# First stage of a decoder trunk on one core: x loaded in four pieces, the norm by token halves, V begun with two units, scale columns finished on ScalarE

## The chip, the core and the metric

One core of a Trainium2 chip runs the whole program. The metric is the device time of one execution in microseconds (us); of several runs the median counts. Engines are called as the profile calls them: PE (TensorE, matmuls), ACT (ScalarE), DVE (VectorE), POOL (GpSimd), SP (SyncE, which issues all DMAs here). They run side by side, each through its own list of instructions in order, and meet only at semaphores.

## What is computed

Two layers of a decoder on x (512 tokens, 1024 features), float32. Cut to what the change touches:

```
mod = c_act @ w_ada[l] + b_ada[l]           # c_act = silu(c); gives sh1, sc1, g1, sh2, sc2, g2
h = rms_norm(x, norm1_g[l]) * (1.0 + sc1) + sh1
proj = h @ w_in[l]                          # conv parts, q, k, v, gate
...                                         # convolution, retention, output projection, MLP
```

with `rms_norm(x, g) = x * rsqrt(mean(x*x) + EPS) * g`. Everything after the first h is unchanged.

## The kernel before

**Layout.** x lies transposed in SBUF: 128 partitions of features, 8 tiles k of 128 features (KT = 8), 512 tokens. A float32 product is made of three matmuls of rounded parts: each operand is split in a high part (a cast to fp32r, on ACT) and a low part (full minus high, a subtraction), and high*high, high*low and low*high are added up in PSUM. So a weight block w_raw[:, j] (128x1024, four slots j, called units) needs a cast to w_hi on ACT and a subtraction to w_lo on DVE or POOL before PE can use it.

**First stage.** The SP queue loads, in order: c and the identity, x in two pieces of 1 MB (`load_x`), bias and parameters between them, then blocks of 512 KB: the modulation weights of tile 0 (scale, shift), the weight units 0 and 1, the scale block of tile 1, the units 2 and 3, the shift block of tile 1, and then scale and shift of the tiles 2 to 7. After the last it waits until all four w_lo are done before it issues the second round of weights.

**Norm.** ACT squares the eight tiles of x (L756), DVE adds them up in `ssum` (L1170), PE takes the mean over features (L386, four small matmuls), ACT the root (L706), DVE the reciprocal (L1217), ACT writes it as diagonal blocks (L788), and PE spreads it over all partitions (L393) into the bank `rinv` of PSUM. Between the fourth and the fifth square ACT copies c_act out of PSUM (L760); POOL's and DVE's work on the modulation waits for that.

**h, tile by tile.** For tile k, DVE multiplies the scale block with c and sums it (L1177, 128x1024), forms the gain from it (L1184), and multiplies x, gain and rinv into `xr` in PSUM (L1194). The shift block is multiplied on POOL (L1584; of tile 0 on DVE, L1213) and summed on ACT (L769, L772). ACT adds the shift and rounds to h_hi (L779), DVE forms h_lo (L1199). In a loop DVE's order is product(k), scale(k+1), gain(k+1), low(k), as `xr` is a single buffer.

**V.** PE begins with V: for each tile k, four token tiles t times three matmuls of 512 columns, all four units at once (`v_tile`, L402 to L404), into the banks 0 to 3. It waits for all four w_lo and for h_lo of tile k. Tile 7 comes in two passes of two units (256 columns). Then the other projections follow (L360 to L362), whose weights are split meanwhile.

**The four weight splits** of the first round: the casts on ACT (L764), the subtractions of units 0, 1 and 3 on POOL (L1579) and of unit 2 on DVE (L1207). POOL has its seven shift blocks behind them.

What sets the order around the change is the text of each engine's list; nothing is scheduled by a planner.

## Time and profile before

| | us |
|---|---|
| median of 3 runs (1164.0 to 1164.42) | 1164.42 |
| the profiled execution | 1164.55 |
| its span, first to last instruction | 1162.6 |
| PE busy | 1133.8 |
| DVE busy | 847.9 |
| ACT busy | 564.2 |
| POOL busy | 183.7 |

The profile is of one execution. The span leaves out 1.95 us (1164.55 less 1162.6) around it. PE is busy for 98% of the span; what it lacks lies almost wholly in the first of 40 slices. A busy share is an average, so the stage in question is read instruction by instruction.

### The profile page before, as it was taken

The page shows a single profiled execution, that of the slowest core. Times are in us where ns is not written, and L with a number is a line of the kernel's source. Part 1 is how long each engine was busy: PE and PEld are TensorE (multiplying, and loading weights), DVE is VectorE, ACT ScalarE, POOL GpSimd, SP SyncE. Part 2 cuts the span into 40 slices and gives each one's busy share as a digit, 9 for nine tenths or more (in the row PEclk, how much of TensorE's full clock was granted, in tenths as well). Part 3 has the DMA queues.
Part 4 walks back from the last instruction along what each step waited for, and adds up shares of the span by engine and source line. Part 5 has one row for each costly group of instructions (what it writes and reads, how often), then busy time and mean ns, then how long its engine had stood idle before and what let it go on. Part 6 is the DMA issues. An engine that isn't in the chain of part 4 may idle for free.

```text
span 1162.6 us, 18883 instructions
## 1 busy us (share of the span) xinstructions
PE 1133.8 (98%) x6650; PEld 1003.3 (86%) x6650; DVE 847.9 (73%) x1275; ACT 564.2 (49%) x941; POOL 183.7 (16%) x140
## 2 busy tenths in 40 slices
PE   4999999999999999999999999999999999999996
PEld 2788888998989989989998888889989989999896
DVE  6966887779778687685577678786897575775754
ACT  5654444347445454454444544434555454544631
POOL 4495010320000000000215801004000000000003
PEclk9999999999999999999999999999999999999998
DMA  9774334624443353433345433452323232232312
GB/s 351 305 289 145 126 108 145 217 74 136 137 159 113 128 161 126 143 114 104 128 158 214 162 126 121 150 204 98 118 101 127 85 109 97 90 126 72 109 54 73
DMA packets 47059, 162.84 MB, mean 140 GB/s; under 512 B 5536, under 2 KB 7712, under 8 KB 46752
## 3 DMA queue, kind: packets, MB, share of 16 engines
q1 hardware_dynamic: 47008, 162.18, 40.4%
q8 instruction: 30, 0.49, 0.2%
q14 instruction: 21, 0.17, 0.0%
HBM read 160.06 MB, written 2.10 MB: 139 GB/s over the span
## 4 chain that ended last, share of the span: by engine, by line
PE 93%; DVE 3%; ACT 1%; DMA 1%; issue 1%; SPq 1%; POOL 0%; POOLq 0%; DVEq 0%; ACTq 0%
PE ps L360 21%; PE ps L361 21%; PE ps L362 21%; PE ps L516 8%; PE ps L518 8%; PE ps L517 8%; PE ps L611 1%; PE ps L402 1%; DVE h_lo L1068 1%; PE ps L596 1%; DMA w_raw<-weights 1%; PE ps L403 1%; PE ps L404 1%; DVE x L1105 1%; DVE x L1133 0%
## 5 line engine op out<-in xcount | busy, mean ns | idle before, releaser
L989 DVE TENSOR_TENSOR w_lo<-w_raw,w_hi 128x1024 fp32r<-128x1024 f32 (+1 forms) x190 | 226.8, 1195 | 195.1 <-ACT w_hi L691 193.5
L691 ACT CAST w_hi<-w_raw 128x1024 fp32r<-128x1024 f32 (+1 forms) x190 | 189.2, 997 | 80.5 <-PE ps L362 69.5
L360 PE MATMUL ps<-u_hi,w_hi 128*128 128x512 f32 (+1 forms) x576 | 211.4, 367 | 0.0
L361 PE MATMUL ps<-u_lo,w_hi 128*128 128x512 f32 (+1 forms) x576 | 210.8, 366 | 0.0
L362 PE MATMUL ps<-u_hi,w_lo 128*128 128x512 f32 (+1 forms) x576 | 210.5, 365 | 0.0
L360 PE MATMUL ps<-h_hi,w_hi 128*128 128x512 f32 (+1 forms) x528 | 194.6, 368 | 0.8 <-DVE h_lo L1068 0.8
L362 PE MATMUL ps<-h_hi,w_lo 128*128 128x512 f32 (+1 forms) x528 | 192.0, 364 | 0.0
L361 PE MATMUL ps<-h_lo,w_hi 128*128 128x512 f32 (+1 forms) x528 | 191.9, 364 | 0.0
L1566 POOL TENSOR_TENSOR ssum<-ssum,buf_a 128x256 f32<-128x256 f32 (+1 forms) x56 | 51.9, 926 | 772.0 <-ACT buf_a L719 769.2
L1133 DVE SCALAR_TENSOR_TENSOR x<-ps,mod,x 128x512 f32<-128x512 f32 (+1 forms) x168 | 105.4, 668 | 35.6 <-PE ps L362 35.6
L362 PEld LDWEIGHTS ps<-u_hi,w_lo 128*128 128x128 f32 x576 | 108.7, 189 | 17.7
L360 PEld LDWEIGHTS ps<-u_hi,w_hi 128*128 128x128 f32 x576 | 108.7, 189 | 16.9
L361 PEld LDWEIGHTS ps<-u_lo,w_hi 128*128 128x128 f32 x576 | 108.8, 189 | 16.6
L360 PEld LDWEIGHTS ps<-h_hi,w_hi 128*128 128x128 f32 x528 | 99.6, 189 | 16.9 <-DVE h_lo L1068 1.6
L362 PEld LDWEIGHTS ps<-h_hi,w_lo 128*128 128x128 f32 x528 | 99.6, 189 | 15.8
L361 PEld LDWEIGHTS ps<-h_lo,w_hi 128*128 128x128 f32 x528 | 99.7, 189 | 15.1
L887 ACT CAST s_hi<-s_full 128x512 fp32r<-128x512 f32 x104 | 63.3, 619 | 75.8 <-DVE s_full L1381 73.4
L516 PE MATMUL ps<-t_hi,s_hi 128*128 128x256 f32 x312 | 88.4, 283 | 0.0
L518 PE MATMUL ps<-t_hi,s_lo 128*128 128x256 f32 x312 | 88.3, 283 | 0.0
L517 PE MATMUL ps<-t_lo,s_hi 128*128 128x256 f32 x312 | 88.3, 283 | 0.0
L1000 DVE CUSTOM_DVE_ANT_0 ada_raw<-ada_raw,c_act 128x1024 f32<-128x1024 f32 x56 | 68.6, 1241 | 3.3 <-DMA ada_raw<-ada 2.9
L1385 DVE TENSOR_TENSOR s_lo<-s_full,s_hi 128x512 fp32r<-128x512 f32 x104 | 66.7, 683 | 0.0
(189 smaller groups left out, 2282.4 us busy)
## 6 DMA issues: line engine op xcount, KB each, us to landing
w_raw<-weights SPq DMA_DIRECT2D x200, 512.0 KB, 3.4
ada_raw<-ada SPq DMA_DIRECT2D x80, 512.0 KB, 4.8
arena<-ada SPq DMA_DIRECT2D x16, 512.0 KB, 15.2
x<-xT SPq DMA_DIRECT2D x2, 1024.0 KB, 6.8
tab<-tables SPq DMA_DIRECT2D x2, 1024.0 KB, 14.6
outT<-x SPq DMA_DIRECT2D x8, 256.0 KB, 2.3
tab<-tables SPq DMA_DIRECT2D x1, 512.0 KB, 14.9
ident<-identity SPq DMA_DIRECT2D x1, 64.0 KB, 2.0
```

Of the source, the lines that this page charges most:

```text
L360: nc.tensor.matmul(out, wh, hi, start=first, stop=False, skip_group_check=True)
L361: nc.tensor.matmul(out, wh, lo, start=False, stop=False, skip_group_check=True)
L362: return nc.tensor.matmul(out, wl, hi, start=False, stop=last, skip_group_check=True)
L516: nc.tensor.matmul(out, wh, high(k), start=first and k == 0, stop=False, skip_group_check=True)
L517: nc.tensor.matmul(out, wh, low(k), start=False, stop=False, skip_group_check=True)
L518: mm = nc.tensor.matmul(out, wl, high(k), start=False, stop=k == 3, skip_group_check=True)
L691: nc.scalar.copy(w_hi[:, j, cols], w_raw[:, j, cols]).then_inc(w_hi_done, 1)
L887: nc.scalar.copy(s_hi[:, at, :], s_full[:, at, :]).then_inc(s_hi_done, 1)
L989: nc.vector.tensor_tensor(w_lo[:, j, cols], w_raw[:, j, cols], w_hi[:, j, cols].bitcast(F32), ALU.subtract).then_inc(w_lo_done, 1)
L1000: nc.vector.tensor_tensor_reduce(out=ada_raw[:, slot, :], in0=ada_raw[:, slot, :], in1=by, scale=1.0, scalar=0.0, op0=ALU.mult, op1=ALU.ad ...
L1133: nc.vector.scalar_tensor_tensor(out=xm, in0=ps[:, bank, at], scalar=mod[:, bass.ds(m + gate_col, 1)], in1=xm, op0=ALU.mult, op1=ALU.add). ...
L1385: nc.vector.tensor_tensor(s_lo[:, at, :], s_full[:, at, :], s_hi[:, at, :].bitcast(F32), ALU.subtract).then_inc(s_split, 1)
```

## The change

x comes in four pieces of two tiles (512 KB), and the host lays it out so that a partition's two tiles are contiguous (4 KB runs instead of 2 KB). The shift block of tile 1 is loaded ahead of the units 2 and 3.

The last two tiles of x are squared and added in halves of 256 tokens, and mean, root, reciprocal, diagonal and spreading are done for each half. The diagonal is now written by DVE (`first_diag`, a multiplication of the identity with the reciprocal, both in SBUF), where ACT did it. The c_act copies move behind the last square on ACT.

POOL begins with the shift block of tile 0, does the subtraction of unit 0 only, and goes on with the shifts of the tiles 1 to 7. DVE does the subtractions of the units 1, 2 and 3, between the steps of the tiles 0 to 2, and no longer the shift block of tile 0. The gains of the tiles 1 to 7 are formed on ACT from the sum (`first_gain`).

Tile 0 of h is made by halves, with its product in SBUF (`xr_first`), not in PSUM. PE does the tiles 0 and 1 of V for the units 0 and 1 first (256 columns, as soon as w_lo of these two is there: `first_lo`), then, when all four are there, the same tiles for the units 2 and 3, then the tiles 2 to 7 as before. SP waits for `first_lo` too before the second round of weights.

```diff
-        xr = ps[:, STAT, :]
+        pair_banks = ps[:, STAT:RMS + 1, :].rearrange("p a t -> p (a t)")
+        first_rinv_all = pair_banks[:, T // 2:T // 2 + T]
+        first_rinv_at = [first_rinv_all[:, at] for at in HALVES]
+        first_stats = [pair_banks[:, 0:2], pair_banks[:, T + T // 2:T + T // 2 + 2]]
+        xr = ps[:, STAT:RMS + 1, :].rearrange("p a (h t) -> p (a h) t", h=2)[:, ::3, :]
+        xr_first = buf_a[:, 0, :]
...
-                sp.dma_start(x[:, 4 * i:4 * i + 4, :], xT[4 * i:4 * i + 4, :, :].rearrange("k p t -> p k t")
-                             ).then_inc(x_in[i], 16)
+                sp.dma_start(x[:, 2 * i:2 * i + 2, :], xT[:, 2 * i:2 * i + 2, :]).then_inc(x_in[i], 16)
...
-            load_x(0)
-            sp.dma_start(bia[:], bias).then_inc(par_in, 16)
-            sp.dma_start(par[:], params).then_inc(par_in, 16)
-            load_x(1)
+            def load_first(j):
+                sp.dma_start(w_raw[:, j, :], weights[j, :, :]).then_inc(w_in[j], 16)
+
+            for i in range(4):
+                load_x(i)
+                if i == 1:
+                    sp.dma_start(bia[:], bias).then_inc(par_in, 16)
+                    sp.dma_start(par[:], params).then_inc(par_in, 16)
             load_scale(0)
             load_shift(0)
-            for j in range(SLOTS):
-                sp.dma_start(w_raw[:, j, :], weights[j, :, :]).then_inc(w_in[j], 16)
-                if j == 1:
-                    load_scale(1)
-            for k in range(1, KT):
+            load_first(0)
+            load_first(1)
+            load_scale(1)
+            load_shift(1)
+            load_first(2)
+            load_first(3)
+            for k in range(2, KT):
+                load_scale(k)
                 load_shift(k)
-                if k + 1 < KT:
-                    load_scale(k + 1)
             sp.dma_start(fin_g[:], final_g).then_inc(fin_in, 16)
+            sp.wait_ge(first_lo, 2)
...
-            pe.wait_ge(x_added, KT - 1)
-            mean_squares(0, 0, 0, TOKEN_TILES)
-            spread(0, 1, WHOLE)
+            for half in range(2):
+                pe.wait_ge(x_added, KT - 1 + 2 * half)
+                for i in range(2):
+                    t = 2 * half + i
+                    mm = nc.tensor.matmul(first_stats[half][:, i:i + 1], ssum[:, t * P:(t + 1) * P], mean_d[:],
+                                          start=True, stop=True, skip_group_check=True)
+                mm.then_inc(stat_ps if half else first_stat, 1)
+            for half in range(2):
+                pe.wait_ge(norm_r if half else first_r, 2)
+                nc.tensor.matmul(first_rinv_at[half], ones[:], ssum[:, HALVES[half]], start=True, stop=True,
+                                 skip_group_check=True).then_inc(rinv_ps if half else first_rinv, 1)
             pe.wait_ge(c_ready, 2)
             pe.wait_ge(mean_ready, 1)
 
+            pe.wait_ge(first_lo, 2)
+            for t in range(TOKEN_TILES):
+                if t % 2 == 0:
+                    pe.wait_ge(xs_lo, t // 2 + 1)
+                v_tile(0, t, (0, 2), True, False)
+            pe.wait_ge(xs_lo, 4)
+            for t in range(TOKEN_TILES):
+                v_tile(1, t, (0, 2), False, False)
             pe.wait_ge(w_lo_done, 2 * SLOTS)
             for k in range(KT):
                 pe.wait_ge(xs_lo, 2 * k + 2)
                 if k < KT - 1:
                     for t in range(TOKEN_TILES):
-                        v_tile(k, t, (0, SLOTS), k == 0, False)
+                        v_tile(k, t, (2 if k < 2 else 0, SLOTS), False, False)
...
+            act.wait_ge(x_in[3], 16)
+            for half, at in enumerate(HALVES):
+                for m in (KT - 2, KT - 1):
+                    act.wait_ge(x_added, m - 4 + 2 * half)
+                    first_square(m, (m + 2 * half) % 4, at)
+            for i in range(2):
+                act.wait_ge(c_ps, i + 1)
+                nc.scalar.copy(c_act[:, HALVES_D[i]], ps[:, 6 + i, :]).then_inc(c_ready, 1)
...
+            def first_gain(k):
+
+                act.wait_ge(sc_summed, k + 3)
+                nc.scalar.activation(gm[:, 0, k:k + 1], sc_sum[:, k:k + 1], ACT.Identity, bias=sc_gain[:, k:k + 1],
+                                     scale=par[:, C_G1 + k:C_G1 + k + 1]).then_inc(gm_ready, 1)
+
             act.wait_ge(par_in, 32)
+            for half in range(2):
+                act.wait_ge(stat_ps if half else first_stat, 1)
+                nc.scalar.activation(std[:, 2 * half:2 * half + 2], first_stats[half], ACT.Sqrt, bias=eps[:, 0:1]
+                                     ).then_inc(norm_std if half else first_std, 1)
             first_split(0)
+            first_shift(0)
             first_split(1)
-            norm_root(0, 1, TOKEN_TILES)
-            act.wait_ge(norm_r, 1)
-            for t in range(TOKEN_TILES):
-                diag = nc.scalar.activation(ssum[:, t * P:(t + 1) * P], ident[:], ACT.Copy, scale=rstd[:, t:t + 1])
-            diag.then_inc(norm_r, 1)
+            act.wait_ge(sh_ready, 1)
+            for half, at in enumerate(HALVES):
+                act.wait_ge(xr_ready if half else first_xr, 1)
+                nc.scalar.activation(h_hi[:, 0, at], xr_first[:, at], ACT.Identity, bias=mod[:, 0:1]).then_inc(xs_hi, 1)
+            first_gain(1)
             first_split(2)
+            first_shift(1)
+            first_high(1)
             first_split(3)
-            first_high(0)
-            for k in range(1, KT):
+            for k in range(2, KT):
+                first_gain(k)
                 first_shift(k)
                 first_high(k)
...
+            for half, at in enumerate(HALVES):
+                for i in range(2):
+                    dve.wait_ge(x_squared, KT - 1 + 2 * half + i)
+                    dve.wait_ge(x_added, KT - 3 + 2 * half + i)
+                    nc.vector.tensor_tensor(ssum[:, at], ssum[:, at], squared[(2 + i + 2 * half) % 4][:, at], ALU.add
+                                            ).then_inc(x_added, 1)
...
+            def first_diag(half):
+
+                step = norm_r if half else first_r
+                t0 = 2 * half
+                dve.wait_ge(norm_std if half else first_std, 1)
+                nc.vector.reciprocal(rstd[:, t0:t0 + 2], std[:, t0:t0 + 2]).then_inc(step, 1)
+                dve.wait_ge(step, 1)
+                nc.vector.tensor_tensor(ssum[:, HALVES[half]].rearrange("p (a b) -> p a b", b=P),
+                                        ident[:].unsqueeze(1).to_broadcast([P, 2, P]),
+                                        rstd[:, t0:t0 + 2].unsqueeze(2).to_broadcast([P, 2, P]), ALU.mult
+                                        ).then_inc(step, 1)
...
+            dve.wait_ge(sc_summed, 1)
+            nc.vector.tensor_tensor(sc_gain[:], sc_bias[:], par[:, C_G1:C_G1 + KT], ALU.mult).then_inc(sc_summed, 1)
+            dve.wait_ge(c_ready, 2)
             first_scale(0)
-            first_gain(0)
-            dve.wait_ge(sh_in[0], 16)
-            nc.vector.tensor_tensor_reduce(out=arena[:, 0, :], in0=arena[:, 0, :], in1=c_row,
-                                           scale=1.0, scalar=0.0, op0=ALU.mult, op1=ALU.add,
-                                           accum_out=sh_sum[:, 0:1]).then_inc(sh_summed, 1)
-            dve.wait_ge(norm_std, 1)
-            nc.vector.reciprocal(rstd[:], std[:]).then_inc(norm_r, 1)
-            dve.wait_ge(sh_summed, 1)
-            nc.vector.tensor_scalar(mod[:, 0:1], sh_sum[:, 0:1], bia[:, 0:1], None, ALU.add).then_inc(sh_ready, 1)
+            first_diag(0)
+            first_diag(1)
+            dve.wait_ge(sc_summed, 3)
+            nc.vector.tensor_scalar(gm[:, 0, 0:1], sc_sum[:, 0:1], sc_bias[:, 0:1], par[:, C_G1:C_G1 + 1],
+                                    ALU.add, ALU.mult).then_inc(gm_ready, 1)
+            dve.wait_ge(gm_ready, 1)
+            for half, at in enumerate(HALVES):
+                dve.wait_ge(rinv_ps if half else first_rinv, 1)
+                nc.vector.scalar_tensor_tensor(out=xr_first[:, at], in0=x[:, 0, at], scalar=gm[:, 0, 0:1],
+                                               in1=first_rinv_at[half], op0=ALU.mult, op1=ALU.mult
+                                               ).then_inc(xr_ready if half else first_xr, 1)
             first_scale(1)
-            first_gain(1)
-            first_split(2)
-            first_product(0)
-            first_low(0)
-            for k in range(1, KT):
+            for half, at in enumerate(HALVES):
+                dve.wait_ge(xs_hi, half + 1)
+                nc.vector.scalar_tensor_tensor(out=h_lo[:, 0, at], in0=xr_first[:, at], scalar=mod[:, 0:1],
+                                               in1=h_hi[:, 0, at].bitcast(F32), op0=ALU.add, op1=ALU.subtract
+                                               ).then_inc(xs_lo, 1)
+            first_split(1, first_lo)
+            first_product(1)
+            first_split(2, w_lo_done)
+            first_low(1)
+            first_scale(2)
+            first_split(3, w_lo_done)
+            for k in range(2, KT):
                 first_product(k)
                 if k + 1 < KT:
                     first_scale(k + 1)
-                    first_gain(k + 1)
                 first_low(k)
...
+            pool.wait_ge(c_ready, 2)
+            first_shift(0)
             first_split(0)
-            first_split(1)
-            first_split(3)
-            pool.wait_ge(c_ready, 2)
             for k in range(1, KT):
...
-        "xT": np.asarray(x)[0].T.reshape(KT, P, T),
+        "xT": np.asarray(x)[0].T.reshape(KT, P, T).transpose(1, 0, 2),
```

Where instructions stand now. The list of POOL before, from its first weight subtraction on (L1579 subtraction of a unit, L1584 shift block of a tile):

```order
L1579 TENSOR_TENSOR w_lo<-w_raw,w_hi 128x1024 [waits w_hi_done] x3
L1584 TENSOR_TENSOR arena<-arena,c_act 128x1024 [waits sh_in1,c_ready]
L1584 TENSOR_TENSOR arena<-arena,c_act 128x1024 [waits sh_in2]
L1584 TENSOR_TENSOR arena<-arena,c_act 128x1024 [waits sh_in3]
L1584 TENSOR_TENSOR arena<-arena,c_act 128x1024 [waits sh_in4]
```

and of the changed kernel (L1656 shift block, L1651 subtraction of unit 0):

```order
L1656 TENSOR_TENSOR arena<-arena,c_act 128x1024 [waits sh_in0,c_ready]
L1651 TENSOR_TENSOR w_lo<-w_raw,w_hi 128x1024 [waits w_hi_done]
L1656 TENSOR_TENSOR arena<-arena,c_act 128x1024 [waits sh_in1]
L1656 TENSOR_TENSOR arena<-arena,c_act 128x1024 [waits sh_in2]
L1656 TENSOR_TENSOR arena<-arena,c_act 128x1024 [waits sh_in3]
```

Two subtractions left POOL, one shift block came, and it stands first.

The list of DVE before, from the first scale block to the product of tile 1 (L1177 scale block, L1184 gain, L1213 shift block, L1207 subtraction of unit 2, L1194 product, L1199 low part):

```order
L1177 ISA arena,sc_sum<-arena,ps 128x1024 [waits sc_in0,c_ready]
...
L1213 ISA arena,sh_sum<-arena,ps 128x1024 [waits sh_in0]
L1213 ISA sh_sum 128x1
L1217 RECIPROCAL rstd<-std 128x4 [waits norm_std]
...
L1184 TENSOR_SCALAR gm<-sc_sum,sc_bias,par 128x1 [waits sc_summed]
L1207 TENSOR_TENSOR w_lo<-w_raw,w_hi 128x1024 [waits w_hi_done]
L1194 SCALAR_TENSOR_TENSOR ps<-x,gm,ps 128x512 [waits gm_ready,rinv_ps]
L1199 SCALAR_TENSOR_TENSOR h_lo<-ps,mod,h_hi 128x512 [waits xs_hi]
L1194 SCALAR_TENSOR_TENSOR ps<-x,gm,ps 128x512 [waits gm_ready,xs_lo]
```

and of the changed kernel, from the second diagonal on (L1243 diagonal half, L1283 product half and L1289 low half of tile 0, L1232 scale block, L1251 subtraction, L1259 product, L1265 low part):

```order
L1243 TENSOR_TENSOR ssum<-ident,rstd 128x256 [waits norm_r]
...
L1283 SCALAR_TENSOR_TENSOR buf_a<-x,gm,ps 128x256 [waits first_rinv,gm_ready]
L1283 SCALAR_TENSOR_TENSOR buf_a<-x,gm,ps 128x256 [waits rinv_ps]
L1232 ISA arena,sc_sum<-arena,ps 128x1024 [waits sc_in1]
...
L1289 SCALAR_TENSOR_TENSOR h_lo<-buf_a,mod,h_hi 128x256 [waits xs_hi] x2
L1251 TENSOR_TENSOR w_lo<-w_raw,w_hi 128x1024 [waits w_hi_done]
L1259 SCALAR_TENSOR_TENSOR ps<-x,gm,ps 128x2x256 [waits gm_ready]
L1251 TENSOR_TENSOR w_lo<-w_raw,w_hi 128x1024 [waits w_hi_done]
L1265 SCALAR_TENSOR_TENSOR h_lo<-ps,mod,h_hi 128x512 [waits xs_hi]
L1232 ISA arena,sc_sum<-arena,ps 128x1024 [waits sc_in2]
...
L1251 TENSOR_TENSOR w_lo<-w_raw,w_hi 128x1024 [waits w_hi_done]
```

Three subtractions now stand between DVE's steps of the tiles 0 to 2, where one stood, and the diagonal and the low halves of tile 0 read two SBUF operands.

## Rows read from the trace of the kernel before

**Rows 1.** The page: PE's busy tenths in 40 slices, and the chain by engine.
```profile
PE   4999999999999999999999999999999999999996
...
PE 93%; DVE 3%; ACT 1%; DMA 1%; issue 1%; SPq 1%; POOL 0%; POOLq 0%; DVEq 0%; ACTq 0%
```

**Rows 2.** Timeline, first 25 us (start us, us, engine, line, operation [idle before <-releaser]).
```profile
9.61 1.05 ACT L760 COPY c_act<-ps 128x512 f32<-128x512 f32 x2
...
10.88 2.15 ACT L756 ACTIVATE ps<-x 128x512 f32<-128x512 f32 x4 [0.21 <-DMA x<-xT]
...
11.51 3.06 DVE L1170 TENSOR_TENSOR ssum<-ssum,ps 128x512 f32<-128x512 f32 x4 [0.49 <-ACT ps L756]
...
14.78 1.04 ACT L764 CAST w_hi<-w_raw 128x1024 fp32r<-128x1024 f32 x1 [1.75 <-DMA w_raw<-weights]
...
18.79 2.08 PE L393 MATMUL ps<-ssum,ones 128*128 128x512 f32 x2 [2.29 <-ACT ssum L788]
...
24.12 0.77 PE L402 MATMUL ps<-w_hi,h_hi 128*128 128x512 f32 x1 [3.25 <-DVE h_lo L1199]
```

**Rows 3.** Timeline: DVE instructions beside POOL instructions, two places.
```profile
15.90 4.67 POOL L1579 TENSOR_TENSOR w_lo<-w_raw,w_hi 128x1024 fp32r<-128x1024 f32 x2 [15.45 <-ACT w_hi L764]
15.94 1.21 DVE L1213 CUSTOM_DVE_ANT_0 arena<-arena,ps 128x1024 f32<-128x1024 f32 x1
...
19.71 1.95 DVE L1207 TENSOR_TENSOR w_lo<-w_raw,w_hi 128x1024 fp32r<-128x1024 f32 x1 [0.74 <-ACT w_hi L764]
...
20.97 2.90 POOL L1579 TENSOR_TENSOR w_lo<-w_raw,w_hi 128x1024 fp32r<-128x1024 f32 x1 [0.39 <-ACT w_hi L764]
...
239.08 2.40 POOL L1571 TENSOR_TENSOR w_lo<-w_raw,w_hi 128x1024 fp32r<-128x1024 f32 x1 [5.70 <-ACT w_hi L691]
239.40 2.37 DVE L1068 SCALAR_TENSOR_TENSOR h_lo<-xr_all,mod,h_hi 128x256 fp32r<-128x256 f32 x1 [0.18 <-ACT h_hi L712]
```

**Rows 4.** All eight diagonal halves on DVE, by line: duration ns min/median/max.
```profile
L1041 DVE TENSOR_TENSOR ssum<-ident,rstd x8: 424/424/715, 235.8 to 1154.9; 128x256 f32<-128x256 f32 x8
```

**Rows 5.** Two shift loads by line, tiles 0 and 2: issue, then landing.
```profile
L282 SPq DMA_DIRECT2D arena<-ada x1: 451/451/451, 4.4 to 4.4; - x1
...
DMA to landing us min/median/max: 9.0/9.0/9.0
...
L282 SPq DMA_DIRECT2D arena<-ada x1: 527/527/527, 8.8 to 8.8; - x1
...
DMA to landing us min/median/max: 14.8/14.8/14.8
```

**Rows 6.** Busy time by window, last columns: PE clock granted, DMA share, GB/s.
```profile
6.50:7.00 0.50, 0.50 (x2) 0.17 (x1) 0.00 (x0) 0.00 (x0) 0.00 (x0) 1.00 1.04 336
...
11.00:11.50 0.50, 0.00 (x0) 0.00 (x0) 0.03 (x1) 0.50 (x2) 0.00 (x0) 1.00 1.00 410
```

**Rows 7.** Timeline, 25 to 50 us: PE's steps and one DVE product and gain.
```profile
25.54 0.63 PE L402 MATMUL ps<-w_hi,h_hi 128*128 128x512 f32 x1
25.97 0.63 PE L403 MATMUL ps<-w_lo,h_hi 128*128 128x512 f32 x1
...
32.30 0.76 DVE L1194 SCALAR_TENSOR_TENSOR ps<-x,gm,ps 128x512 f32<-128x512 f32 x1
32.31 0.50 PE L402 MATMUL ps<-w_hi,h_hi 128*128 128x512 f32 x1
...
34.22 0.27 DVE L1184 TENSOR_SCALAR gm<-sc_sum,sc_bias,par 128x1 f32<-128x1 f32 x1
...
43.87 0.50 PE L402 MATMUL ps<-w_hi,h_hi 128*128 128x512 f32 x1
44.21 0.40 PE L403 MATMUL ps<-w_lo,h_hi 128*128 128x512 f32 x1
...
46.72 0.28 PE L402 MATMUL ps<-w_hi,h_hi 128*128 128x256 f32 x1
...
49.59 0.40 PE L360 MATMUL ps<-h_hi,v_hi 128*128 128x512 f32 x1
```

64 lines of the change are left out of this document (30 added, 34 removed).

## The prediction

> **What bounds the kernel now.** I read the page first: PE is at nine tenths in every slice but the first and the last, and makes up 93% of the chain that ended last [rows 1]. So nothing after the first 50 us can be won by this change, and what the first stage gains or loses passes through whole, as a shift. The measure of the stage is the moment at which PE leaves V and starts the next projection: 49.59 us [rows 7]. Then the timeline of the first 25 us: the last four squares start at 10.88, when the second half of x has landed, the last sum is ready at 14.57 (11.51 + 3.06), the spreading ends at 20.87, V begins at 24.12 after 3.25 us of idle PE [rows 2]. Then V itself: matmuls of 512 columns come every 0.43 us at first (25.54 to 25.97: the 1.2 GHz level) and every 0.228 later (44.21 to 46.72 for eleven of them: the 2.4 GHz level). Tile 2 begins at 32.31 and tile 7 at 46.72, so a tile takes 2.88, though PE needs only 12 x 0.228 = 2.74 [rows 7]: DVE paces it, by 0.14 per tile.
>
> **Which resource decides.** Two places show DVE and POOL standing in each other's way. At 239.40 DVE's low half takes 2.37 us while a POOL subtraction runs from 239.08 to 241.48, and ends 0.29 after it; all eight diagonal halves lie between 0.424 and 0.715 us, so 0.47 is what such an instruction needs alone [rows 3, 4]. At 19.71 DVE's subtraction takes 1.95 and ends 1.09 after POOL's second one (15.90 + 4.67 = 20.57); POOL's third then takes 2.90 instead of 2.34 and ends 2.21 after DVE's [rows 3]. But DVE's block product at 15.94, which has one operand in PSUM, takes 1.21 in the middle of a POOL instruction [rows 3]. So: a DVE instruction with two SBUF inputs waits for the running POOL instruction to end, and POOL's next waits for it. Reading from these rows, a held subtraction ends 1.1 after POOL's end, and POOL's next ends 2.2 after that. The changed kernel gives DVE three such subtractions, two diagonals and two low halves at a time in which POOL, with its shift blocks first, is hardly idle. That is the heart of this prediction.
>
> **Part 1, the loads.** While x comes in, the queue moves 336 GB/s at a full DMA share, and 410 later [rows 6]. x's runs become as long as the other blocks'. The 2.1 MB of x take 6.2 us at the one rate and 5.1 at the other, so all that follows lands between 0 and 1.1 us earlier; I take 0.8, nearer the later row, because the later blocks have just these runs. The last of x then lands at 10.1 instead of 10.88. Shift block 0 landed at 4.4 + 9.0 = 13.4 and shift block 2 at 8.8 + 14.8 = 23.65 [rows 5]; their places in the queue stay, so 12.6 and 22.85.
>
> **Part 2, the norm.** After x's last piece there were four squares and sums left, 3.7 us to the last sum. Now four halves: a sum of 512 columns takes 0.77 (3.06 / 4), a half about 0.43 (a diagonal half's 0.424, [rows 4]), and DVE is still at the fifth sum until 11.0. So the first half's sum is ready at 11.9 and the second's at 12.7. Mean and root end at 14.15 for the second half (an estimate: about 0.95 for two of the four small matmuls, 0.3 for the root). The c_act copies, 1.05 us [rows 2], now stand last on ACT and end at 12.5, which costs nothing, since shift block 0 lands at 12.6.
>
> **Part 3, the chain through POOL.** POOL's shift 0 runs 12.6 to 15.0. DVE's scale 0 ends at 14.1; its first diagonal is ready at 14.2, is held and ends at 15.3. ACT casts unit 0 from 14.15 to 15.2 (1.04, [rows 2]), so POOL takes its subtraction at 15.2, and DVE's second diagonal asks at 15.4, too late by about 0.2: it ends at 17.9, not 15.8. Spreading a half: 1.04 to 2.08, half of the whole's 2.08 [rows 2] or all of it; I take 1.2, as its columns halve. It ends at 19.1, the second product half at 19.7, scale 1 at 20.8, both low halves at 21.6, DVE's subtraction of unit 1 at 22.7 (POOL is idle here: shift 1 done at 20.2, shift 2 not landed). V begins at 22.8, 1.3 earlier than now.
>
> **Part 4, the chain to the second pair of units.** DVE makes product 1 (0.76, [rows 7]) until 23.4 and then asks for the subtraction of unit 2. POOL began shift 2 at 22.9, when it landed, and ends at 25.2. The subtraction ends at 26.3, POOL's shift 3 at 28.5. Low 1 ends at 27.0, scale 2 at 28.1, the subtraction of unit 3 is held until 28.5 and ends at 29.6. Only then are all four w_lo there. PE: tile 0 for two units, 12 steps of half 0.43, 22.8 to 25.3; idle; tile 1 at 27.05 to 29.6 at the low clock; the second pair from 29.7. Its 24 steps of 0.12 ((49.59 - 46.72) / 24, [rows 7]) are 2.87, and 0.3 more for what is still at the low clock, so tile 2 begins at 32.9. That is 0.6 **later** than the 32.31 of now, though V began 1.3 earlier.
>
> **Part 5, the gains on ACT.** They take 0.27 from DVE's loop [rows 7]; its 2.88 falls to 2.6 or 2.7, below PE's 2.74. The next limit is PE itself. ACT has 2.5 us of work per tile with it (an estimate from its shift, high and gain steps), which is below 2.74. Five tiles at 2.74 are 13.7 instead of 14.41, a gain of 0.7; without this cover being complete the gain lies between 0 and 0.7. Tile 7 keeps its 2.87.
>
> **Part 6, the second round of weights.** SP waits now until 29.6 (it issued at 23.9), but blocks landed 15 us after their issue [rows 5], so the queue is filled to about 36 and the wait costs nothing; it would cost from a wait until 34 on.
>
> **The sum.** 32.9 + 13.7 + 2.87 = 49.5 against 49.59: **-0.1 us**. The profiled execution has 1164.55, of which 1.95 outside the span; it lies 0.13 above the median, 1164.42. On the median's side: 1164.3, rounded to **1164.4**, no change. What moves it inside this case: the loads 0 to 1.1 earlier (+0.8 to -0.3), the gain's cover (+0.7 to 0), the clock in the idle places (-0.3 to +1.2).
>
> **Rival A, the order flips.** In Part 4 DVE asks 0.4 us after POOL has begun shift 2, in Part 3 0.2 us after POOL has begun unit 0. If DVE comes first at the second place (or at the first, which brings the spreading 2 us forward and DVE most of the 0.4), the subtraction of unit 2 ends at 24.5, shift 2 at 26.7, low 1 at 25.2, scale 2 at 26.4, and the subtraction of unit 3 at 27.8. The second pair starts at 27.85 at full clock and tile 2 at 30.7: 2.3 earlier than in the forecast, so 1162.1. For it: both margins are smaller than what the estimates of Part 2 and 3 leave open. Against: both would have to be wrong in the same direction, as the landings shift both sides alike. Chance 0.24, half of it beyond 0.2%.
>
> **Rival B, no waiting.** If these operands don't hold DVE, subtractions end where they are asked for: unit 1 at 20.6, unit 3 at 25.4, tile 2 at 28.4, 4.5 earlier than in the forecast: 1159.9. Against it stand rows 3 and 4. The Trainium skill speaks for waiting too: "SBUF — State Buffer", "Who interferes with whom", says that a DVE instruction with two SBUF inputs contends with a GpSimd one that reads SBUF and that the order of issue decides who blocks. By that rule this rival falls and the forecast or rival A is left. Chance 0.05.
>
> **Rival C, slower: PE's clock falls back.** V's start now has two idle places, 1.7 us after tile 0 and, if tile 1 runs at the high level, 1.2 before the second pair. Before, it had one of 0.74 behind tile 0, and stayed at the high level after it, which it reached 3.2 us after V began. The point from which it decides is whether PE is still at the low level at 29.7. Then a climb of 3.2 us at half speed costs 1.6, of which 0.3 is in the sum: +1.2, 1165.6; with loads that gain nothing besides, +2.0; only a second climb brings it past 0.2%. The Trainium skill ("TensorE: Matmul & The Clock Gate", "What's actually happening") has the low rate as the default that activity releases; by it the three short bursts are a worse start than one long one. No row shows what 1.7 us of idle do. Chance 0.12, of which 0.06 past 0.2%.
>
> **Rival D.** That the change does not do what it says, for instance x in 4 KB runs out of a source with a longer pitch between them gaining nothing or losing: then all lands as now and the time is 1165.1. It is inside the forecast's own range.
>
> **How the numbers follow.** Forecast case 0.59, with its own range of 1163.5 to 1165.6; A 0.24 at 1162.1; C 0.12 at 1165.6 and up; B 0.05 at 1159.9. A measurement of this kernel can tell about 0.2% (2.3 us) from no change. Faster by more: half of A, B and a rest, 0.20. Slower by more: 0.06. Same: 0.74. For 8 in 10 the range takes in most of A and of C: 1161.7 to 1166.0.
>
> **What would show it.** In the profile of the changed kernel: V's first matmul near 22.8; DVE subtractions of the units 2 and 3 of more than 1.9 us each, ending just behind POOL shift blocks; the second diagonal held by more than 1.5 us; the second pair's first matmul (256 columns) near 29.7; tile 2 near 32.9 and then tiles of 2.74; the next projection at 49.5. Rival A shows the subtraction of unit 2 at its 1.2 us and POOL's shift 2 longer instead. B shows three subtractions of 1.2. C shows steps of 0.21 us for 256 columns after 30. I would be wrong, too, if PE were seen waiting again between the tiles 3 and 7, or if the loads of x landed later than 10.9.

## The result, and the profile after

| | before | changed |
|---|---|---|
| median, 15 runs each (us) | 1164.42 (1163.75 to 1164.83) | 1170.99 (1165.76 to 1172.93) |
| ratio, 95% interval | | 1.0058 (1.0051 to 1.0065) |
| the profiled execution | 1164.55 | 1172.48 |
| its span | 1162.6 | 1170.7 |

**Slower by 0.58%.** The forecast was no change, and the range ended at 1166.0, so it was wrong. The runs of the changed kernel lie in two groups, 1170.4 to 1171.1 and 1172.2 to 1172.9, and one at 1165.76; the profile is of the upper one. What parts them stays open.

The page of the changed kernel: PE's tenths and the granted clock in 40 slices, and the chain by engine.

```profile
PE   2999999999999999999999999999999999999996
...
PEclk6899999999999999999999999999999999999998
...
PE 93%; DVE 5%; ACT 1%; DMA 1%; issue 0%; SPq 0%; POOL 0%; POOLq 0%; DVEq 0%; ACTq 0%
```

As in [rows 1], all but the first slice is PE's. That slice fell from 4 to 2 tenths, and DVE's part of the chain rose from 3% to 5%. So the place to look is the first 50 us, and DVE in it. The timeline of that stretch, changed kernel (start us, us, engine, line, operation [idle before <-releaser]):

```profile
10.97 1.30 ACT L786 ACTIVATE ps<-x 128x256 f32<-128x256 f32 x4 [0.19 <-DMA x<-xT]
...
13.64 2.34 POOL L1656 TENSOR_TENSOR arena<-arena,c_act 128x1024 f32<-128x1024 f32 x1 [13.20 <-DMA arena<-ada]
13.80 2.22 DVE L1270 TENSOR_SCALAR sc_bias<-bia 128x8 f32<-128x8 f32 x1
...
17.52 1.37 DVE L1243 TENSOR_TENSOR ssum<-ident,rstd 128x256 f32<-128x256 f32 x1
...
19.00 2.37 DVE L1243 TENSOR_TENSOR ssum<-ident,rstd 128x256 f32<-128x256 f32 x1
...
23.81 2.35 POOL L1656 TENSOR_TENSOR arena<-arena,c_act 128x1024 f32<-128x1024 f32 x1 [2.72 <-DMA arena<-ada]
...
24.23 4.77 DVE L1289 SCALAR_TENSOR_TENSOR h_lo<-buf_a,mod,h_hi 128x256 fp32r<-128x256 f32 x2
26.38 2.34 POOL L1656 TENSOR_TENSOR arena<-arena,c_act 128x1024 f32<-128x1024 f32 x1 [0.22 <-DMA arena<-ada]
28.92 1.21 DVE L1251 TENSOR_TENSOR w_lo<-w_raw,w_hi 128x1024 fp32r<-128x1024 f32 x1
...
30.39 0.55 PE L419 MATMUL ps<-w_hi,h_hi 128*128 128x256 f32 x1 [7.74 <-DVE w_lo L1251]
30.71 2.76 DVE L1251 TENSOR_TENSOR w_lo<-w_raw,w_hi 128x1024 fp32r<-128x1024 f32 x1
...
35.20 1.60 DVE L1251 TENSOR_TENSOR w_lo<-w_raw,w_hi 128x1024 fp32r<-128x1024 f32 x1
...
40.59 0.40 PE L419 MATMUL ps<-w_hi,h_hi 128*128 128x512 f32 x1
```

What to see, in order:

- The squares behind the last piece of x start at 10.97, where they started at 10.88 [rows 2].
- **sc_bias**, eight numbers per partition out of one SBUF tile, takes 2.22 us. It begins 0.16 after POOL's shift block and ends 0.04 after it (16.02 to 15.98). Nothing in the prediction speaks of it. In the kernel before it stood between the sums, with POOL idle until 15.90 [rows 3]:

```profile
10.86 0.16 DVE L1166 TENSOR_SCALAR sc_bias<-bia 128x8 f32<-128x8 f32 x1
```

- Scale block and diagonals follow two microseconds late, and the second diagonal is held to 21.37 by shift block 1.
- The two **low halves** of tile 0 ask at 24.23. Shift block 2 has started at 23.81, so the first is held to 26.2, and shift block 3 holds the second to 29.0. Together they take 4.77 us; where nothing holds them they take 0.88 (e1 below).
- V starts at 30.39 instead of 24.12 [rows 2], after 7.74 us of idle PE. Subtractions of the units 2 and 3 are held too. Tile 2 starts at 40.59 instead of 32.31, and V is left at 57.09 instead of 49.59 [rows 7]: **7.5 us later**. The span grew by 8.1; the other 0.6 lies behind V.

Busy time by window of the changed kernel; the last three columns are the granted PE clock, the DMA share and GB/s:

```profile
28.00:32.00 4.00, 1.61 (x7) 1.64 (x8) 4.00 (x4) 1.12 (x2) 3.78 (x2) 0.50 1.03 410
32.00:36.00 4.00, 3.10 (x15) 2.80 (x14) 4.00 (x5) 1.20 (x3) 4.00 (x3) 0.50 0.78 304
36.00:40.00 4.00, 4.00 (x26) 3.98 (x25) 3.96 (x7) 3.09 (x7) 4.00 (x2) 0.68 0.52 181
```

DVE is busy for all of 28 to 36 and PE is not; DVE's held instructions count as busy. The PE clock is at its lower level, 1.2 GHz, up to the third of these windows, and V's steps of 256 columns came every 0.21 us until about 38.5, then every 0.12. The DMA queue begins to run dry behind 32 (its share falls to 0.78, then 0.52), as SP waits for the last w_lo and issues the second round at 36.88.

### The profile page after: what moved, and what is told of

It is laid out like the page before. It is cut to its first block, busy times and chain, and to the rows that moved or that the text cites. A ratio compares the mean times of both kernels' runs of the same rounds, so it can differ in the third digit from the quotient of the medians.

```text
span 1170.7 us, 18946 instructions
## 1 busy us (share of the span) xinstructions
PE 1135.7 (97%) x6676; PEld 1007.8 (86%) x6676; DVE 859.5 (73%) x1275; ACT 567.3 (48%) x951; POOL 183.5 (16%) x139
## 4 chain that ended last, share of the span: by engine, by line
PE 93%; DVE 5%; ACT 1%; DMA 1%; issue 0%; SPq 0%; POOL 0%; POOLq 0%; DVEq 0%; ACTq 0%
PE ps L377 21%; PE ps L378 21%; PE ps L379 21%; PE ps L533 7%; PE ps L535 7%; PE ps L534 7%; PE ps L644 1%; PE ps L419 1%; DVE h_lo L1121 1%; PE ps L420 1%; PE ps L421 1%; PE ps L629 1%; DMA x<-xT 1%; DVE x L1158 1%; DVE x L1186 0%
```

## The experiments

**Theory H:** POOL holds DVE. One small instruction, sc_bias, was held where the prediction counted nothing, and that pushed the low halves under the shift blocks 2 and 3. **Rivals:** the low clock of PE at V's start; the shape of V's start (two units first). A profile is of one execution, which can lie a microsecond or more beside its kernel's median; where that matters it is said. All kernels were compared with the kernel before on the same chip, whose median lay between 1164.24 and 1164.48 in every comparison.

### One part undone at a time

**e1**: sc_bias and sc_gain stand before the fourth sum.

```diff
             for m in range(1, KT - 2):
+                if m == 4:
+                    dve.wait_ge(par_in, 32)
+                    nc.vector.tensor_scalar(sc_bias[:], bia[:, 1:2 * KT:2], 1.0, None, ALU.add).then_inc(sc_summed, 1)
+                    ...
                 dve.wait_ge(x_squared, m + 1)
...
-            dve.wait_ge(par_in, 32)
-            nc.vector.tensor_scalar(sc_bias[:], bia[:, 1:2 * KT:2], 1.0, None, ALU.add).then_inc(sc_summed, 1)
```

> The changed kernel, with the two small DVE instructions for sc_bias and sc_gain back ahead of the fifth sum, where POOL is idle. Theory (a DVE instruction whose operands need the path shared with POOL waits for the running POOL instruction): sc_bias takes 0.16 us instead of 2.22, the diagonals are asked for 2 us earlier but the second is still held, V starts at 23.5 to 24.5 instead of 30.4 because the low halves now come before shift 2 lands, PE leaves V at about 51 instead of 57.1; time 1166. Rival (the stage is longer because of the loads or of the low PE clock alone): V starts 0 to 2 us earlier than 30.4, time 1170 to 1173.

Measured: 1165.69, ratio 1.0008 (0.9998 to 1.0018). Its timeline:

```profile
9.62 0.17 DVE L1219 TENSOR_SCALAR sc_bias<-bia 128x8 f32<-128x8 f32 x1
...
22.12 0.88 DVE L1290 SCALAR_TENSOR_TENSOR h_lo<-buf_a,mod,h_hi 128x256 fp32r<-128x256 f32 x2
...
24.15 2.38 POOL L1657 TENSOR_TENSOR arena<-arena,c_act 128x1024 f32<-128x1024 f32 x1 [2.67 <-DMA arena<-ada]
24.39 0.55 PE L419 MATMUL ps<-w_hi,h_hi 128*128 128x256 f32 x1 [3.84 <-DVE w_lo L1256]
```

Moving two instructions of 0.17 us gave 5.3 of the 6.6 us back (1165.69 against 1170.99, by medians). The low halves now ask at 22.12, two microseconds before shift block 2, and take 0.88. Tile 2 starts at 34.25 and V is left at 50.75.

**e2**: tile 0's product lies in PSUM, so that the low halves have one SBUF input.

```diff
-        xr_first = buf_a[:, 0, :]
+        xr_first = [pair_banks[:, 0:T // 2], pair_banks[:, T + T // 2:2 * T]]
```

> The changed kernel, with the product of tile 0 in PSUM, so that the two low halves of tile 0 read one SBUF operand. Theory: they take 0.48 us each instead of 4.77 together; the subtraction of unit 1 may be held once instead; V starts 3 to 5 us earlier, at 25.5 to 27.5, and PE leaves V near 54; time 1167 to 1169. Rival (the halves were long for another reason, such as waiting for ACT): they stay above 2 us.

Measured: 1168.66, ratio 1.0040 (1.0025 to 1.0054); V starts at 27.48 and is left at 53.92.

```profile
23.79 2.35 POOL L1655 TENSOR_TENSOR arena<-arena,c_act 128x1024 f32<-128x1024 f32 x1 [2.62 <-DMA arena<-ada]
...
24.30 0.87 DVE L1288 SCALAR_TENSOR_TENSOR h_lo<-ps,mod,h_hi 128x256 fp32r<-128x256 f32 x2
25.09 2.13 DVE L1251 TENSOR_TENSOR w_lo<-w_raw,w_hi 128x1024 fp32r<-128x1024 f32 x1
```

Asked at nearly the same moment as in the changed kernel (24.30 and 24.23), both low halves take 0.87 with POOL running: with an operand in PSUM they aren't held. The hold goes to the subtraction behind them.

**e3**: the diagonals are written by ACT, the reciprocals come before scale block 0.

```diff
+                for t in (2 * half, 2 * half + 1):
+                    diag = nc.scalar.activation(ssum[:, t * P:(t + 1) * P], ident[:], ACT.Copy, scale=rstd[:, t:t + 1])
...
-                nc.vector.tensor_tensor(ssum[:, HALVES[half]].rearrange("p (a b) -> p a b", b=P),
-                                        ...
```

> The changed kernel, with the two diagonals written by ACT (two instructions of 128 columns for each half) and the reciprocals ahead of the first scale block on DVE. Theory: no diagonal is held, spreading is done at 18.5 instead of 22.65; then the subtraction of unit 1 or the low halves meet shift 2 and V starts at 24 to 27.5, PE leaves V between 51 and 54; time 1166 to 1169. Rival: V starts within 1 us of 30.4.

Measured: 1169.85, ratio 1.0046 (1.0029 to 1.0062). V starts at 28.04 and is left at 55.04, later than expected.

```profile
21.83 2.67 DVE L1289 SCALAR_TENSOR_TENSOR h_lo<-buf_a,mod,h_hi 128x256 fp32r<-128x256 f32 x2 [0.49 <-ACT h_hi L844]
...
24.33 2.37 POOL L1656 TENSOR_TENSOR arena<-arena,c_act 128x1024 f32<-128x1024 f32 x1 [0.51 <-DMA arena<-ada]
...
24.42 3.36 DVE L1251 TENSOR_TENSOR w_lo<-w_raw,w_hi 128x1024 fp32r<-128x1024 f32 x1
```

The low halves meet shift block 1 now, and the subtraction of unit 1 comes 0.09 after shift block 2 has started. A hold that is taken away is followed by the next one. The edit has a price of its own too: ACT's diagonals stand ahead of its cast of unit 0, POOL waited 2.63 us for that cast, and shift block 1 started at 21.47 instead of 18.69.

**e5**: e1, e2 and e3 together.

> The changed kernel with all three edits at once: sc_bias and sc_gain early, the diagonals on ACT, the product of tile 0 in PSUM. Theory: only the three weight subtractions on DVE can still be held; V starts between 23.2 and 24.5 instead of 30.4, PE leaves V between 47.8 and 49 (49.59 before the change), time 1162.5 to 1164. Rival (the edits are worth no more together than the best of them alone, which left V at 50.75): time 1165 or more.

Measured: 1163.82, ratio 0.9995 (0.9986 to 1.0005). In the profile V starts at 23.43 but is left at 49.95, not at 49 or before; all three subtractions are still held (2.33, 3.33 and 1.62 us). The profiled execution, 1164.92, is 1.1 above the median.

### Is POOL the cause?

**e4**: POOL writes the shift blocks' product area without reading (the shift is left out of h).

```diff
-                nc.gpsimd.tensor_tensor(arena[:, 2 * k, :], arena[:, 2 * k, :], c_act[:], ALU.mult
-                                        ).then_inc(sh_product, 1)
+                nc.gpsimd.memset(arena[:, 2 * k, :], 0.001).then_inc(sh_product, 1)
```

> The changed kernel, with POOL's eight shift products replaced by plain writes of the same blocks (the shift is then left out of the result), so that POOL reads no SBUF there. Theory: every DVE instruction of the first stage goes back to its own duration (sc_bias 0.16, diagonals 0.42, low halves 0.48, subtractions 1.2), except beside POOL's one subtraction; V starts near 21.6, PE leaves V near 46 to 47; time 1161 to 1162. Rival (writes hold DVE too, or the waits come from elsewhere): the long durations stay and V starts after 27.

Measured: 1163.05, ratio 0.9987 (0.9978 to 0.9997); V starts at 23.71 and is left at 48.09.

```profile
13.19 0.95 POOL L1656 MEMSET arena<- 128x1024 f32 x1 [12.74 <-DMA arena<-ada]
13.39 0.78 DVE L1270 TENSOR_SCALAR sc_bias<-bia 128x8 f32<-128x8 f32 x1
...
23.36 0.95 POOL L1656 MEMSET arena<- 128x1024 f32 x1 [4.16 <-DMA arena<-ada]
...
24.03 1.22 DVE L1251 TENSOR_TENSOR w_lo<-w_raw,w_hi 128x1024 fp32r<-128x1024 f32 x1
```

All three subtractions take 1.22 now. Only the one shown met a memset: they share 0.28 us, and it wasn't held. The whole loss, and more, hangs on POOL's eight shift blocks; as they are also shorter here (0.95 instead of 2.35), the run doesn't say how much is the reading and how much the length. V starts later than the 21.6 expected, since the second diagonal met POOL's subtraction of unit 0 and took 2.38 us. And sc_bias is held even by an instruction that only writes: it ends 0.03 after the memset.

### Which forms are held

**e11** and **e13** add DVE instructions of 128x8 whose results nobody uses.

```diff
+                if k == 2:
+                    nc.vector.tensor_scalar(probe[:, 0:KT], bia[:, 1:2 * KT:2], 1.0, None, ALU.add)
+                    ...
```

> The changed kernel with five DVE instructions of 128x8 elements more, whose results nobody uses, beside POOL's row of shift blocks (about 28 to 42 us): two behind the product of tile 2 (add of a constant, with a source of every second element, as sc_bias; the same with a contiguous source), three behind the product of tile 3 (add and multiply with scalars per partition; a plain copy; a product of two SBUF tiles). Alone each takes about 0.17 us. The theory that POOL holds every form that DVE can run at its fast rate or that has two SBUF inputs expects the two adds of a constant, the copy and the product of two tiles to be held up to 2.3 us (ending with a POOL instruction), and the form with scalars per partition perhaps not, as the gains of 128x1 took 0.27. The rule on which the prediction rested expects only the product of two tiles to be held. A third theory, that the source of every second element is slow, expects only the first.

Measured, one run: 1172.59. The first, sc_bias over again, took 1.72 us at 37.12, with POOL running. The second stood right behind it (0.16), and the other three came after POOL's last shift block had ended at 41.15 (0.28, 0.17, 0.16). Inconclusive for these four; so e13 puts its forms where POOL runs for certain:

```diff
+            dve.wait_ge(sh_in[0], 16)
+            dve.wait_ge(c_ready, 2)
+            nc.vector.tensor_scalar(probe[:, 2 * KT:3 * KT], bia[:, 0:KT], eps[:, 0:1], eps[:, 0:1], ALU.add, ALU.mult)
+            nc.vector.tensor_copy(probe[:, 3 * KT:4 * KT], bia[:, 0:KT])
             nc.vector.tensor_scalar(sc_bias[:], bia[:, 1:2 * KT:2], 1.0, None, ALU.add).then_inc(sc_summed, 1)
...
             first_scale(0)
+            nc.vector.tensor_scalar(probe[:, KT:2 * KT], bia[:, 0:KT], 1.0, None, ALU.add)
```

> The changed kernel with three DVE instructions of 128x8 more whose results nobody uses: in front of sc_bias, just after POOL has begun shift block 0, an add and multiply with scalars per partition and a plain copy; behind scale block 0, where POOL does the subtraction of unit 0, an add of a constant with a contiguous source. If all forms with one SBUF input and no scalar per partition are held: the first takes 0.28 us, the copy about 2 (ending with POOL's shift block near 16.0), sc_bias behind it 0.17, and the contiguous add more than 1, ending near 18.6 with POOL's subtraction. If only a source of every second element is held: copy and contiguous add take 0.17 each, sc_bias between them 1.9. If scalars per partition are held too, the first one takes 2.2 and the copy 0.17.

Measured, one run: 1171.47.

```profile
14.00 2.35 POOL L1662 TENSOR_TENSOR arena<-arena,c_act 128x1024 f32<-128x1024 f32 x1 [13.55 <-DMA arena<-ada]
14.17 2.21 DVE L1273 TENSOR_SCALAR probe<-bia,eps 128x8 f32<-128x8 f32 x1
16.29 0.16 DVE L1274 COPY probe<-bia 128x8 f32<-128x8 f32 x1
...
16.62 2.36 POOL L1657 TENSOR_TENSOR w_lo<-w_raw,w_hi 128x1024 fp32r<-128x1024 f32 x1 [0.27 <-ACT w_hi L805]
...
17.84 1.17 DVE L1280 TENSOR_SCALAR probe<-bia 128x8 f32<-128x8 f32 x1
```

The form with scalars per partition and a contiguous source is held (to 16.38, POOL's end 16.35), and so is the add of a constant with a contiguous source (to 19.01, POOL's end 18.98). Neither the stride nor the kind of scalar matters. The copy fell between two POOL instructions and tells nothing. A gain of 128x1, the same kind of instruction with one element, took 0.27 beside POOL's shift blocks [rows 7] and 0.26 in e1 (19.19, POOL from 19.03). So what is held is this form with one SBUF input, at eight elements but not at one; where the hold begins no run shows. The Trainium skill has the eight elements: "VectorE: DVE Perf Modes", "What auto-detection actually checks", has a one-source instruction whose source and result lie in SBUF take a mode of two ports if the outermost non-unit dimensions are both even or equal, and "SBUF — State Buffer", "Who interferes with whom", names `tensor_scalar` in that mode among those that contend with GpSimd. The runs with eight elements agree (2.21 and 1.17 us in e13).

### The clock as rival

**e7** puts five dummy matmuls on PE ahead of V in the kernel before, **e8** fourteen in the changed kernel, **e6** five in e5. One or more stand before the spreading, the rest behind it; the second part of e6's edit:

```diff
+            for _ in range(4):
+                nc.tensor.matmul(ps[:, 0, HALVES[0]], ones[:], x[:, 0, HALVES[0]], start=True, stop=True,
+                                 skip_group_check=True)
             pe.wait_ge(c_ready, 2)
```

> The kernel before, with five such added matmuls, two between the means and the spreading and three behind it. Theory: tile 0 of V (12 steps) takes 2.8 us instead of 4.6, but tile 1 then waits for DVE, whose h_lo of tile 1 is ready at 29.4 as before: gain 0 to 0.3 us, time 1164.1 to 1164.5. Rival (the low clock is what bounds the start of V): gain 1.6 us, time 1162.8.

Measured: 1164.97, ratio 1.0005 (0.9995 to 1.0014). V ran at the high level from its start (0.23 us per 512 columns instead of 0.43) and was left at 49.64 all the same: DVE's tile 1 (29.42) set the pace.

> The changed kernel, with fourteen such added matmuls, four before the spreading and ten behind it. Theory (the waits of DVE set V's times, not the clock): V starts at 30.4 as before, the second pair of units still at 36.9, when its last w_lo is there; only the seven steps after 36.9 that were at the low rate get faster, PE leaves V about 0.8 us earlier than at 57.1; time 1170 to 1172. Rival (the low clock until 38.5 is the main loss): PE leaves V 3 us earlier or more, time below 1169.

Measured: 1172.73, ratio 1.0073 (1.0056 to 1.0089). A miss: the dummies ended at 26.2, V started at 30.02, its steps were 0.21 again, and it was left at 57.24. What the clock alone costs the changed kernel was not measured. An estimate from its trace is 0.8 us: PE was done with tile 1 at 36.92, the last w_lo was there at 36.80, and the 24 steps up to tile 2 took 3.67 us (36.92 to 40.59) instead of 24 times 0.12. e8 shows the holds from another side: the low halves asked 0.08 before shift block 2 (23.50 and 23.58) and took 2.99 instead of 4.77, and then the subtraction of unit 1 took 3.35, so V began no more than 0.4 earlier.

> As e5, with five added float32 matmuls whose results are thrown away, one between the means and the spreading and four behind it, so that PE is not idle before V. Theory (V's first steps at 0.21 us per 256 columns are at the low clock only because PE stood idle before): V starts as in e5, its steps take 0.12 from the start, and PE leaves V 0.5 to 1.6 us earlier than in e5. Rival (the low rate at the start of V has nothing to do with idle): same exit as e5, or later.

Measured: 1162.92, ratio 0.9987 (0.9977 to 0.9996). In the profile V's first eight steps took 0.12 and the later ones up to 30.8 took 0.21 again; V was left at 49.98, as in e5. The granted clock, third from the right, agrees:

```profile
22.00:24.00 2.00, 0.87 (x7) 0.90 (x8) 2.00 (x3) 1.65 (x4) 0.64 (x1) 1.00 1.02 408
24.00:26.00 2.00, 1.26 (x7) 0.96 (x5) 2.00 (x1) 1.24 (x2) 1.83 (x2) 0.52 1.03 412
```

But this execution took 1164.52, and eight of the ten lie at 1162.45 to 1163.16. The median is 0.9 below that of e5 on the same chip (1163.82), inside the 0.5 to 1.6 that the theory expected. So the profile shows a fall that can happen; the usual execution was faster, and of that one there is no trace.

### The useful parts alone, on the kernel before

**e9**: x in four pieces of 4 KB runs, nothing else.

> The kernel before with only the loading of x changed: four pieces of 512 KB in runs of 4 KB, squares two by two. It leaves nothing out. The prediction's Part 1 wants the last of x at 10.1 us instead of 10.88. The rival, read from the profile of the changed kernel (last piece at 10.97), is that the length of the runs gains nothing: the last piece lands at 10.9 again. In either case only two squares are then left after the last piece instead of four, so the spreading should begin about 1.3 us before 18.79, at 17.5, or at 16.7 by Part 1. V then begins at most 1 us before 24.12, as DVE still has the subtraction of unit 2 in front of the product: leaving V at 48.6 to 49.6, and 1163.4 to 1164.4 in all by the rival, 0.8 less by Part 1.

Measured: 1164.18, ratio 0.9999 (0.9990 to 1.0008). The last of x lands at 10.6 (issue at 4.0, 6.6 to the landing; in the kernel before issue at 3.2 and 7.7, so 10.9).

```profile
14.60 1.04 ACT L765 CAST w_hi<-w_raw 128x1024 fp32r<-128x1024 f32 x1 [2.78 <-DMA w_raw<-weights]
...
15.82 1.04 ACT L765 CAST w_hi<-w_raw 128x1024 fp32r<-128x1024 f32 x1 [0.18 <-DMA w_raw<-weights]
16.77 0.26 ACT L707 ACTIVATE std<-ps,eps 128x4 f32<-128x4 f32 x1
```

The sums end at 13.28, 1.3 earlier, but the spreading starts at 18.61 (18.79 before): the root stands behind two casts on ACT that wait for the weights. My expectation of 17.5 overlooked that queue.

**e10**: the gains of the tiles 2 to 7 on ACT, nothing else.

```diff
+                if k > 1:
+                    act.wait_ge(sc_summed, k + 3)
+                    nc.scalar.activation(gm[:, 0, k:k + 1], sc_sum[:, k:k + 1], ACT.Identity, bias=sc_gain[:, k:k + 1],
+                                         scale=par[:, C_G1 + k:C_G1 + k + 1]).then_inc(gm_ready, 1)
                 first_shift(k)
```

> The kernel before with only the gains of tiles 2 to 7 moved from DVE to ACT, as in the change, and sc_gain formed once beside the fourth sum. It leaves nothing out. Part 5 of the prediction: a tile takes 2.74 instead of 2.88 us, V is left 0.7 us earlier (48.9 instead of 49.6) and the time is 1163.7. The rival is that ACT (its gain step took 0.38 in the changed kernel, not 0.27) or DVE's start of tile 2 then paces it: the tiles stay at 2.88 and the time at 1164.4.

Measured: 1163.73, ratio 0.9994 (0.9985 to 1.0003). V is left at 48.91 (48.9 expected). The sign is as expected, but the interval takes in no change.

### Taking the holds away

**e12**: e5 with the subtraction of unit 3 on POOL and tile 1's low part before the subtraction of unit 2; ACT casts unit 3 ahead of its part of shift block 1.

> The kernel with the three edits (scale columns early, tile 0's product in PSUM, diagonals on ACT), in which moreover POOL does the subtraction of unit 3 behind shift block 1, and DVE the low part of tile 1 before the subtraction of unit 2. It leaves nothing out. By the theory that each DVE subtraction beside POOL's shift blocks is held: one hold goes (unit 3), the first one of 3.3 us falls to at most 2.2, tile 1 begins near 26 instead of 27.8, all four w_lo are there near 27, tile 2 begins at 31 instead of 33.4, V is left near 48, and the time is 1162.3. The rival: POOL is now late with shift block 2 (28.1 instead of 26.0) and tile 2 or a later one waits for it; then V is left at 49.5 to 50 as with the three edits, 1163.8.

Measured: 1165.14, ratio 1.0007 (0.9998 to 1.0016). A miss.

```profile
25.37 5.73 POOL L1655 TENSOR_TENSOR arena<-arena,c_act 128x1024 f32<-128x1024 f32 x2
25.51 3.32 DVE L1256 TENSOR_TENSOR w_lo<-w_raw,w_hi 128x1024 fp32r<-128x1024 f32 x1
```

DVE's subtraction came 0.14 after the shift block and was held for its whole length. Then scale block 2 was late, and PE waited 1.45 us for tile 2's low part (33.46). The expectation had at most 2.2 us for it, where it took 3.32.

**e14**: so the work is exchanged, not reordered. POOL takes the subtractions of the units 0, 2 and 3, DVE the shift blocks of the tiles 1 and 2, with c in PSUM. ACT, which no longer sums these two, casts unit 3 ahead of tile 1.

```diff
             first_split(1, first_lo)
+            shift_here(1)
             first_product(1)
-            first_split(2, w_lo_done)
-            first_low(1)
             first_scale(2)
-            first_split(3, w_lo_done)
+            first_low(1)
+            shift_here(2)
...
-            first_split(0)
-            for k in range(1, KT):
+            first_split(0, first_lo)
+            first_split(2, w_lo_done)
+            first_split(3, w_lo_done)
+            for k in range(3, KT):
                 first_shift(k)
```

> The kernel with the three edits, in which DVE and POOL exchange work: POOL does the subtractions of the units 0, 2 and 3 (that of unit 0 and two more in a row) and DVE the shift blocks of the tiles 1 and 2, whose second operand lies in PSUM. It leaves nothing out. Theory (holds are the loss that is left): every DVE instruction behind V's start has its own length, unit 1 1.2 us, shift blocks 1.2 each, all four w_lo are there near 26.7, V starts near 22.3, and PE is the bound: 24 half steps at the low clock (5.1) and 24 at the high one (2.9) with about 0.9 of idle time, so tile 2 begins near 31.3, V is left near 47.8, and the time is 1162.4. Rival (the low clock and the division of V's start in halves are the loss): tile 2 begins near 33 all the same and the time is as with the three edits, 1163.8.

Measured: 1163.68, ratio 0.9993 (0.9984 to 1.0002).

```profile
21.09 1.22 DVE L1256 TENSOR_TENSOR w_lo<-w_raw,w_hi 128x1024 fp32r<-128x1024 f32 x1
21.91 4.95 POOL L1660 TENSOR_TENSOR w_lo<-w_raw,w_hi 128x1024 fp32r<-128x1024 f32 x2 [1.90 <-ACT w_hi L804]
...
30.85 0.41 PE L419 MATMUL ps<-w_hi,h_hi 128*128 128x256 f32 x1
...
33.02 0.40 PE L419 MATMUL ps<-w_hi,h_hi 128*128 128x512 f32 x1
```

No DVE instruction behind V's start is held, and all four w_lo are there at 26.86, as expected. But tile 2 starts at 33.02, as the rival said: V's steps of 256 columns took 0.21 us from 22.56 to 31.7, twice the 0.12 of the high level. So by this profile **the low clock** is what is left once the holds are gone; the next two runs test it. By medians e14 gained nothing that can be told on e5 (1163.68 and 1163.82), and its profiled execution, 1164.71, is 1.0 above its median.

**e15**: e14 with five dummy matmuls ahead of V. **e16**: one more of them, and two with a weight block of zeros between tile 0 and tile 1, which add nothing to V.

```diff
                 v_tile(0, t, (0, 2), True, False)
+            for _ in range(2):
+                nc.tensor.matmul(ps[:, 0, HALVES[0]], zeros[:], x[:, 0, HALVES[0]], start=False, stop=False,
+                                 skip_group_check=True)
             pe.wait_ge(xs_lo, 4)
```

> The same as e14_swap_work with five dummy matmuls of 256 columns on PE ahead of V (one behind the mean, four behind the spreading), whose results nobody uses. If holds were the loss and PE's clock is what is left: steps of 0.12 us from V's start, tile 2 up to 2 us before that of e14_swap_work, limited by the four w_lo (26.7 + 2.9 = 29.6), and 1161 in all. If the clock falls back in V's idle places as in e6_three_undone_warm: within 0.5 us of e14_swap_work.

Measured: 1162.58, ratio 0.9986 (0.9977 to 0.9995); V is left at 48.00. Three windows of e15, PE's clock third from the right:

```profile
24.00:26.00 2.00, 0.39 (x3) 0.39 (x4) 2.00 (x4) 0.92 (x2) 2.00 (x1) 1.00 1.01 401
26.00:28.00 2.00, 2.00 (x14) 2.00 (x14) 1.97 (x5) 0.31 (x1) 2.00 (x2) 0.69 1.05 418
28.00:30.00 2.00, 2.00 (x12) 2.00 (x11) 1.97 (x4) 1.61 (x3) 2.00 (x2) 0.50 1.01 397
```

PE stood idle from 23.6 to 25.61, ran at 0.12 us per step, and then fell to 0.21 at 26.8 while it was busy, until 30.0. That is the 1.2 GHz level again, behind a busy stretch as well as an idle one.

> The same as e15_swap_warm with one dummy matmul more ahead of V (five behind the spreading) and two with a weight block of zeros, which add nothing, on PE between tile 0 and tile 1 of V, where it stood idle for 2 us. If the idle place is what made the clock fall back at 26.8: all half steps of V take 0.12 us, the second pair of units begins near 27.1, tile 2 at 30.0 instead of 31.5, V is left at 46.5 instead of 48.0, and the time is 1161.2. If the clock is low there for another reason: as e15_swap_warm, 48.0 and 1162.6.

Measured: **1162.11, ratio 0.9981 (0.9972 to 0.9990)**, the fastest of these kernels: 0.19% faster than before. e6 and e15 have intervals below 1 too (e4 as well, with its shift left out).

```profile
28.16 0.28 PE L420 MATMUL ps<-w_hi,h_hi 128*128 128x256 f32 x1
...
30.68 0.40 PE L420 MATMUL ps<-w_hi,h_hi 128*128 128x512 f32 x1
...
47.18 0.40 PE L378 MATMUL ps<-h_hi,v_hi 128*128 128x512 f32 x1
```

All half steps took 0.12 us. Counted from V's start, tile 2 begins after 10.46 us in e14 (22.56 to 33.02), 9.53 in e15 (21.97 to 31.50) and 8.06 here (22.62 to 30.68), with tile 1 after 3.64 in all three. So the low level cost 2.4 us in e14's profile and 1.5 in e15's. By medians the steps are smaller: 1163.68, 1162.58 and 1162.11, 1.6 us in all, the last on another chip. V is left at 47.18, 2.4 earlier than in the kernel before; 46.5 and 1161.2 were expected, and V's start 0.65 behind e15's is the difference. What exactly makes the clock fall isn't shown: PE stood idle for 2.20 us ahead of V here, and for 2.33 ahead of tile 1 in e7, and didn't fall; it stood idle for 2.21 ahead of V in e6 and fell 1.0 us later. The third rival, the shape of V's start, is no loss by itself: e16 keeps two units first and leaves V earlier than the kernel before.

## Why the prediction was wrong, step by step

**What bounds the kernel.** Right: nothing behind V mattered much. Of the span's 8.1 us, 7.5 are V's exit. Against the kernel before, span and exit moved together within 0.6 us in every experiment.

**Which resource decides.** Right in kind: DVE against POOL. **The step that failed** is the rule drawn from rows 3 and 4, "a DVE instruction with two SBUF inputs waits". It was read backwards too, as if no other did, and so Part 2 and Part 3 have no term for sc_bias, which has one input. The gains of 128x1 in rows 7 aren't held, but they are one element wide; sc_bias has eight and was held for 2.22 us, and e13 shows two more such forms held, for 2.21 and 1.17.

**Part 1, the loads.** The size was off: 0.8 us earlier was taken, -0.1 measured (10.97), and 0.3 in e9 (10.6). The lower end of the range fits best, and rival D with it. Finer than that it can't be read: with these same loads the squares behind the last piece began anywhere from 10.51 to 11.50 in the profiles of the other kernels, and at 10.86 to 10.97 in the three with the old loads. Shift blocks 0 and 2 began at 13.64 and 23.81, both 1.0 late against the forecast.

**Part 2, the norm.** The root of the second half was forecast for 14.15 and came at 15.24: 0.9 of it from the loads and 0.2 more. What Part 2 left out is the move of sc_bias from between the sums to behind them, where POOL has started. The whole change has that line, but the excerpt ahead of the prediction shows only sc_gain behind it, and the lists of DVE there begin behind it. An edit that seemed to cost 0.17 us was costed at nothing, without a word on what it now stands beside. e1 prices it: **5.3 us** of the 6.6. The other 1.3 weren't taken apart; e1's V begins 1.6 after the forecast's 22.8.

**Part 3, the chain through POOL.** "Low halves done 21.6, not held (POOL is idle here)" was right with sc_bias out of the way (e1: 22.12 to 23.0) and wrong by 7.4 us without. The cover was the gap between shift block 1 and shift block 2, and its edge was 2.05 us away by the forecast's own numbers (22.85 less 20.8), just what sc_bias takes. A cover that ends at a landing should have been given a price for what lies behind it: two low halves, each waiting for a whole shift block. V was forecast for 22.8; it was 24.39 in e1 and 30.39 here.

**Part 4, the second pair.** The pattern was right, shifted: the subtractions of the units 2 and 3 were held (2.76 and 1.60 us; 2.90 and 1.60 in e1), as forecast. The sign "more than 1.9 us each" was set wrong for unit 3, to which Part 4 itself gives 1.5. Tile 2 was forecast for 32.9; e1 has 34.25. All of that stands ahead of the last w_lo, there at 30.93 instead of 29.6; the 24 steps behind it took 3.19 us (31.06 to 34.25), as forecast.

**Part 5, the gains.** Right: tiles 2 to 6 took 2.73 us each (40.59 to 54.22), PE waited for none, and e10 shows the 0.7 us by itself in V's exit.

**Part 6, the second round.** The wait for w_lo lasted to 36.88 instead of 29.6, past the 34 that the prediction named, and the queue ran dry (0.52 of its share at 36 to 40). The 0.6 us behind V don't come from PE waiting for these weights: the waits of PE that the profiles list from 60 us on are the same in both kernels, 5.6 us. Where they come from stays open.

**Rival A** (the order flips at a close call) did happen, but on the other side: close calls were lost, the low halves here by 0.42 us (24.23 against 23.81), a subtraction in e3 by 0.09 and in e12 by 0.14. I had only priced the flips that help. **Rival B** (no waiting) was wrong. **Rival C**, the clock, was right as a mechanism: the steps of 0.21 us after 30 were there. In the changed kernel DVE's waits hid most of it (0.8 us by the estimate at e8); with the holds gone it cost 2.4 us in e14's profile against e16's, and 1.6 by medians.

**The sign.** The slower side had 0.06 with a clock for its reason. The right rival would have been: the low halves miss the gap and wait for two shift blocks, +3.9, and V begins after them. It decides once DVE is 2.05 us late.

## What to carry to other kernels

Where DVE and POOL both work on SBUF, price every DVE instruction that the change puts beside a running POOL instruction, small ones first: eight elements can cost the whole rest of a 2.3 us instruction, and one of them in front of the queue moves all others to where they wait too. Give DVE the work with an operand in PSUM and POOL the work with SBUF operands, rather than tune an order with margins of 0.1 us. That exchange alone was worth nothing that could be told here (e14 against e5); with PE kept at its high clock besides, the kernel ran 2.1 us below the one before. And when a bound is removed, look at the length of PE's steps, not only at when they start: the half speed was the next bound here. Before reading a bound out of a profile, see how far its execution lies from the median: e6's lay 1.6 us above, and its trace alone would have said that the dummies were worth nothing.

## What the runs showed of the hardware

- A one-input DVE instruction of 128x8 in SBUF is held to the end of POOL's running one, read or write (2.22, 2.21, 1.17, 1.72 us; 0.78 beside a memset of 0.95). 128x1 isn't (0.26). A two-input subtraction that shared 0.28 us with a POOL memset wasn't (1.22 in e4). With one of two inputs in PSUM DVE isn't held (0.87 for two low halves in e2).
- The held instructions of 128x8 end 0.03 to 0.04 after POOL's. If POOL's next one is ready, the two take turns, and DVE's next is held again (low halves, 4.77 us for two).
- PE fell from 0.12 to 0.21 us per 256 columns while it was busy, 1.2 us after an idle place of 2.0 us, and came back 3.2 us later (e15). With that place half filled it didn't fall (e16). In e6 it fell 1.0 us after an idle place of 2.21 us; idle places of 2.20 (e16) and 2.33 us (e7) weren't followed by a fall.
- The granted clock of a window can read 1.00 where the steps show the low level. One window of e14, in which the steps of 256 columns came every 0.213 us:

```profile
28.50:31.50 3.00, 3.00 (x16) 3.00 (x16) 2.96 (x5) 2.46 (x6) 3.00 (x2) 1.00 1.02 407
```

- Runs of 4 KB instead of 2 KB moved the last landing of x by +0.1 and -0.3 us, less than the 1.0 us by which it differs between profiles with the same loads.
